# Attention outputs scaled before the transposes, summed in one PSUM group and left transposed

## The chip, the cores and the metric

The kernel runs on one core of a Trainium2 chip. The metric is the device time of one execution in microseconds; lower is better. The engines are TensorE (PE; its weight loads are PEld), VectorE (DVE), ScalarE (ACT), GpSimd (POOL) and SyncE (SP), which issues transfers.

## What is computed

One layer of a decoder on 1024 tokens of width 1024, in float32: a feed-forward, token mixing by attention, a feed-forward, each followed by a normalisation. Of the mixing, what matters here (cut to its core):

```python
# group A, sparse: 8 heads in 2 groups, 64 wide, query tiles of 128; three branches
p_cmp = masked_softmax(qb @ k_cmp * scale)          # 63 compressed keys
p_sel = masked_softmax(qb @ k_sel * scale)          # all blocks up to the tile
p_win = masked_softmax(qb @ kwb * scale)            # the last 512 keys and the tile's own
gates = sigmoid(gate_logits)
o = gates[..., 0:1] * (p_cmp @ v_cmp) + gates[..., 1:2] * (p_sel @ v_sel) + gates[..., 2:3] * (p_win @ vwb)
# group B, latent: 8 heads, queries and keys 96 wide, values 64, causal
p = masked_softmax((qn @ k_nope + qr @ k_rope) * scale)
o = p @ v
# both: the heads' outputs side by side (1024 columns) @ w_out, gated, added to alpha * x
# masked_softmax(s): e = exp(s - max), 0 where masked; e / max(sum(e), 1e-30)
```

## The kernel before

`sparse_attention` and `latent_attention` build lists of units and give them to `attend`. A unit is 512 query rows as four rows of 128 (in the sparse part four heads of one tile, in the latent part four tiles of one head) against its blocks of keys: in the sparse part 48 units (2 groups x 8 tiles x 3 branches, in the order selection, window, compressed), with 1 to 8 blocks of 128 keys for the selection, 1 to 5 for the window and one of 64 for the compressed branch, 132 blocks of 128 in all; in the latent part 16 units (8 heads x 2 halves) with 4 and 8 blocks. For each unit:

- *score*: PE makes the scores in PSUM, DVE their negated maximum, ACT the exponentials into `exps`, with their sums.
- *turn*, once a block: PE transposes the block's exponentials into one of three ring banks (`BANKS`); ACT rounds them into `turned_hi`; DVE subtracts into `turned_lo` (L2805) and so frees the bank.
- *apply*, once a block: PE multiplies the value matrix with `turned_hi` and with `turned_lo` into `out_ps` (L2735). The value matrix holds 64 columns of high parts and 64 of low parts, so `out_ps` has two halves of 64 rows, each an output, transposed.
- *finish*, once a unit: ACT copies `out_ps` to `out_sb` (L2769), PE transposes it back by four transposes into a ring bank (L2741), DVE adds the two halves (L2816) and inverts the floored sums (L2809, L2813), POOL multiplies by the factor, and in the sparse part by the gate, and adds the branch to `h` (L2829 to L2842).

Three rooms hold exponentials in the sparse part, one for each branch, and four in the latent part. POOL also scales the latents' columns in the first 16 units (L2915).

`plan` writes each engine's order by a list schedule: it gives every step a price (`pe_price` and so on), and picks on each engine the head of a stream that can start first; between those that can start equally soon the tuple in the call decides (`"pe": (1, 2, 0, 0)` for scoring, turning, applying, finishing: applying and finishing come first). Each engine then runs its order and waits on semaphores that count steps.

After the latent attention, `modulated_transpose` (stage `turn3`) transposes all of `h`'s 8 output chunks on PE into `u_hi` and `u_lo` for the output projection. `project` then takes `w_out` in chunks of 128 rows: DVE multiplies a chunk by the gate row (L2003), ACT rounds it (L1983), DVE subtracts (L2006), and PE does 8 x 3 matmuls for it (L2044). The chunks and the gate row are requested at the start of `turn3`, the rows of x behind them.

## Time and profile before

| | us |
|---|---|
| median of 3 runs (2226.71 to 2231.69) | 2229.32 |
| the profiled execution, whole | 2232.52 |
| its span | 2230.7 |
| PE busy in the span | 2115.3 (95%) |
| DVE busy | 1508.7 (68%) |
| ACT busy | 1001.9 (45%) |
| POOL busy | 599.0 (27%) |

The sparse attention stands at 924 to 1218 us of the span, the latent inputs at 1218 to 1273, the latent attention at 1273 to 1449, `turn3` at 1449 to 1462, the output projection up to 1554, the second feed-forward behind it. Matmuls are pipelined: an instruction's duration overlaps the next one's, so what one costs PE is better read from start to start. The mean in a row of groups is one instruction's; the busy time beside it counts overlapping parts once.

### The profile page before, as it was taken

Reading aid. Unit: us, or ns where it says so; the run is one execution under the profiler, and the core shown is the slowest. Engines: PE = TensorE matmul, PEld = TensorE weight load, DVE = VectorE, ACT = ScalarE, POOL = GpSimd, SP = SyncE. Lnnn points to the kernel's source line nnn. Section 1 sums busy time; section 2 is a strip of 40 time slices with the busy share of each in tenths; the row PEclk is TensorE's granted clock in tenths of the full one; section 3 lists DMA queues with packets and bytes.
Section 4 is the critical chain, followed back from the end, with each engine's and each line's share of the span. In section 5 each row is a group of like instructions: output and inputs, shape, how many; then the busy total and the mean of one; then the engine's idle time right before and its main releaser. Section 6 shows DMA issues by size and latency. Waiting matters only on the chain. (4 is left out here: it accounts for less than half of the span.)

```text
span 2230.7 us, 29121 instructions
## 1 busy us (share of the span) xinstructions
PE 2115.3 (95%) x10361; PEld 1771.7 (79%) x10361; DVE 1508.7 (68%) x2361; ACT 1001.9 (45%) x1925; POOL 599.0 (27%) x597
## 2 busy tenths in 40 slices
PE   5999999999999999799998899998999999999997
PEld 4888888878887887688886789877788888887885
DVE  6877777766886414687887577744765555558689
ACT  3433333334554112887886467621733323324443
POOL 0366656611100000132312000000245555540301
PEclk9999999999998999799999899989999999999998
DMA  7255544468831310300000000041333333347975
GB/s 268 88 168 170 166 165 162 168 206 267 249 109 56 126 46 18 117 1 1 1 1 1 1 1 1 1 151 36 112 118 113 104 118 109 105 127 259 293 258 100
DMA packets 193638, 254.46 MB, mean 114 GB/s; under 512 B 18192, under 2 KB 116560, under 8 KB 193495
## 3 DMA queue, kind: packets, MB, share of 16 engines
q1 hardware_dynamic: 178088, 208.04, 28.1%
q0 software_dynamic: 15408, 44.57, 7.7%
q8 instruction: 83, 1.36, 0.2%
q14 instruction: 59, 0.48, 0.1%
HBM read 212.72 MB, written 43.52 MB: 115 GB/s over the span
## 5 line engine op out<-in xcount | busy, mean ns | idle before, releaser
L781 DVE TENSOR_TENSOR ffn2A_u<-ffn2A_u,ffn_banks 128x512 f32<-128x512 f32 x60 | 41.2, 687 | 118.5 <-PE ffn_banks L725 112.4
L2757 ACT ACTIVATE nsaa_exps<-nsaa_scores,nsaa_neg_max 128x64 f32<-128x64 f32 (+8 forms) x192 | 108.3, 578 | 23.5 <-DVE nsaa_neg_max L2790 15.1
L2805 DVE TENSOR_TENSOR nsaa_turned_lo<-nsaa_ring,nsaa_turned_hi 128x512 fp32r<-128x512 f32 (+1 forms) x148 | 96.7, 683 | 23.4 <-ACT nsaa_turned_hi L2766 22.2
L1315 DVE SCALAR_TENSOR_TENSOR late_part_late<-ada_rows,far_silu_c,late_part_late 128x1024 f32<-128x1024 f32 x56 | 107.2, 1914 | 3.3 <-DMA ada_rows<-in_w_ada 3.2
L602 ACT ACTIVATE ffn1A_t_hi<-ffn1A_t 128x512 fp32r<-128x512 f32 x80 | 48.5, 628 | 132.2 <-POOL ffn1A_t L595 100.3
L602 ACT ACTIVATE ffn2A_t_hi<-ffn2A_t 128x512 fp32r<-128x512 f32 x80 | 48.4, 628 | 122.1 <-POOL ffn2A_t L595 93.8
L2044 PE MATMUL in_acc<-mix_in_w_hi,mix_in_u_hi 128*128 128x494 f32 x256 | 99.4, 388 | 0.7 <-PEq L85 0.7
L2044 PE MATMUL in_acc<-mix_in_w_lo,mix_in_u_hi 128*128 128x494 f32 x256 | 99.1, 387 | 0.0
L2044 PE MATMUL in_acc<-mix_in_w_hi,mix_in_u_lo 128*128 128x494 f32 x256 | 99.0, 387 | 0.0
L725 PE MATMUL ffn_banks<-ffn1S_s_hi,ffn1A_t_hi 128*128 128x512 f32 x240 | 93.8, 391 | 0.0
L725 PE MATMUL ffn_banks<-ffn1S_s_hi,ffn1A_t_lo 128*128 128x512 f32 x240 | 93.4, 389 | 0.0
L725 PE MATMUL ffn_banks<-ffn2S_s_hi,ffn2A_t_hi 128*128 128x512 f32 x240 | 93.4, 389 | 0.0
L725 PE MATMUL ffn_banks<-ffn1S_s_lo,ffn1A_t_hi 128*128 128x512 f32 x240 | 93.4, 389 | 0.0
L725 PE MATMUL ffn_banks<-ffn2S_s_lo,ffn2A_t_hi 128*128 128x512 f32 x240 | 93.4, 389 | 0.0
L725 PE MATMUL ffn_banks<-ffn2S_s_hi,ffn2A_t_lo 128*128 128x512 f32 x240 | 93.4, 389 | 0.0
L2766 ACT ACTIVATE nsaa_turned_hi<-nsaa_ring 128x512 fp32r<-128x512 f32 (+1 forms) x148 | 83.3, 599 | 20.1 <-PE nsaa_ring L2725 19.3
L2725 PE MATMUL nsaa_ring<-all_ident,nsaa_exps 128*128 128x128 f32 (+1 forms) x592 | 82.9, 275 | 2.7 <-DVE nsaa_turned_lo L2805 2.5
L2006 DVE TENSOR_TENSOR mix_in_w_lo<-mix_in_w_raw,mix_in_w_hi 128x494 fp32r<-128x494 f32 x28 | 18.8, 672 | 97.4 <-ACT mix_in_w_hi L1983 97.4
L619 DVE TENSOR_TENSOR ffn2A_t_lo<-ffn2A_t,ffn2A_t_hi 128x512 fp32r<-128x512 f32 x80 | 73.8, 945 | 13.9 <-ACT ffn2A_t_hi L602 12.9
L781 DVE TENSOR_TENSOR ffn1A_u<-ffn1A_u,ffn_banks 128x512 f32<-128x512 f32 x60 | 41.0, 684 | 58.5 <-PE ffn_banks L725 58.5
L2725 PEld LDWEIGHTS nsaa_ring<-all_ident,nsaa_exps 128*128 128x128 f32 (+1 forms) x592 | 68.1, 138 | 11.0 <-DVE nsaa_turned_lo L2805 4.2
L997 PE MATMUL ffn_banks<-ffn2B_d_hi 128*128 128x512 f32 x188 | 73.6, 392 | 2.5 <-ACT ffn2R_p L1040 1.7
(643 smaller groups left out, 6921.2 us busy)
## 6 DMA issues: line engine op xcount, KB each, us to landing
ada_rows<-in_w_ada POOLq DMA_DIRECT2D x56, 512.0 KB, 4.7
ffn_raw_g<-in_ffn_wg SPq DMA_DIRECT2D x44, 512.0 KB, 3.7
ffn_raw_u<-in_ffn_wu SPq DMA_DIRECT2D x44, 512.0 KB, 4.9
early_w<-in_w_ada SPq DMA_DIRECT2D x16, 512.0 KB, 7.0
mix_in_w_raw<-in_w_in SPq DMA_DIRECT2D x32, 247.0 KB, 2.6
ffn_rest<-in_ffn_wd SPq DMA_DIRECT2D x29, 256.0 KB, 5.0
hidden<-ffn1A_c SPq DMA_DIRECT2D x22, 256.0 KB, 4.5
hidden<-ffn1A_u SPq DMA_DIRECT2D x22, 256.0 KB, 5.0
```

Of the source, the lines that this page charges most:

```text
L602: act.activation(self.b_hi[w][:, :], self.block_of(w), ACT.Copy).then_inc(self.rounded, 1)
L619: dve.tensor_tensor(self.b_lo[w][:, :], self.block_of(w), self.b_hi[w][:, :].bitcast(F32), ALU.subtract).then_inc(self.split, 1)
L725: last = pe.matmul(out, b[w][:, cols], u[a][:, c, :], start=(not joins and c == 0 and m == 0), stop=(c == KC - 1 and m == 2), skip_group_c ...
L781: dve.tensor_tensor(out, base, bank, ALU.add).then_inc(self.mixed, 1)
L997: last = pe.matmul(self.banks[:, 4 * QUAD[p] + i, :], h[:, rows], w[:, HALF:D], start=(j == 0 and at == 0 and not JOINS[p]), stop=(j == PA ...
L1315: dve.scalar_tensor_tensor(out=part_late[:, v, :], in0=ada[:, n % 2, :], scalar=silu_c[:, k:k + 1], in1=part_late[:, v, :], op0=ALU.mult, ...
L2006: dve.tensor_tensor(lo[:, k, :], raw[:, k, :], hi[:, k, :].bitcast(F32), ALU.subtract).then_inc(split, 1)
L2044: last = pe.matmul(acc[:, i, 0:width], u[:, c, i * P:(i + 1) * P], w[:, c % slots, :], start=(c == 0 and m == 0), stop=(c == DC - 1 and m ...
L2725: last = pe.transpose(bank[0:u.keys, r * P:(r + 1) * P], exps[n % slots][:, r, k * u.keys:(k + 1) * u.keys], ident[:, :])
L2757: made = act.activation(u.kept(r, exps[n % slots]), u.seen(r, scores[:, m % 2, :]), ACT.Exp, bias=neg_max[:, n % SUMS, r:r + 1], accum_out ...
L2766: act.activation(turned_hi[0:u.keys, j % copies, cols], bank[0:u.keys, cols], ACT.Copy).then_inc(hi_done, 1)
L2805: dve.tensor_tensor(turned_lo[0:u.keys, j % copies, cols], bank[0:u.keys, cols], turned_hi[0:u.keys, j % copies, cols].bitcast(F32), ALU.s ...
```

## The change

The exponentials of a block are multiplied by their row's factor (1 / sum, in the sparse part gate / sum) in place, before the turn. In the sparse part POOL does every block; in the latent part's long units DVE does the first three blocks (`by_vector`) and POOL the others. The gate goes into the floored sum as 1 + exp(-x), which `sparse_inputs` now makes instead of the sigmoid. So the three branches of a tile add up in one PSUM group. *Finish* is gone; *fold* takes its place, once a tile and group (16 times) or once a latent unit (16 times): ACT copies one half of `out_ps`'s rows across to `other`, and DVE adds the other half and writes the sum, still transposed, into `h`. The compressed branch's values stand twice, on 128 partitions, and the low part of its turned block goes to the lower 64 rows of `turned_hi`, so that one matmul applies both. Each branch has two rooms, some of them unused columns of `h`. `turn3` is gone: `project` makes `u_hi` and `u_lo` from `h` chunk by chunk, and requests the chunks, the gate row and then x itself. The scaling of the latents moves from POOL to DVE. The streams' order on PE becomes scoring, turning, applying.

```diff
-def modulated_transpose(nc, stage, x_sb, shift, scale, ident, u_hi, u_lo, ahead, reload=None, arrives=None):
...
 def project(...):
+            if reload is not None:
+                chunks.ahead(sp)
             load(0, slots)
+            if reload is not None:
+                for i in range(TT):
+                    sp.dma_start(out[:, i, :], reload[i * P:(i + 1) * P, :]).then_inc(out_in[0], 16)
...
+                if u_raw is not None and n == 0:
+                    act.activation(u_hi[:, c, :].rearrange("p (i q) -> p i q", q=P), u_raw[c], ACT.Copy).then_inc(u_hi_done, 1)
...
+                if u_raw is not None and n == 0:
+                    dve.wait_ge(u_hi_done, c + 1)
+                    dve.tensor_tensor(u_lo[:, c, :].rearrange("p (i q) -> p i q", q=P), u_raw[c],
+                                      u_hi[:, c, :].bitcast(F32).rearrange("p (i q) -> p i q", q=P), ALU.subtract).then_inc(u_split, 1)
...
 def plan(...):
         elif kind == "turn":
-            found.append(("act", last_score[n]))
+            found.append(("dve" if k < u.by_vector else "pool", ("weigh", n, u.weighed_with(k))))
         elif kind == "apply":
             found.append(("dve", ("turn", n, k)))
-            if k == 0 and n:
-                found.append(("act", ("apply", n - 1, len(units[n - 1].blocks) - 1)))
-            if is_last(x) and n:
-                found.append(("pe", ("finish", n - 1, 0)))
+            if k == 0 and u.opens and u.group:
+                found.append(("dve", fold_of[u.group - 1]))
...
 def attend(...):
-                    if k == 0 and n:
-                        pe.wait_ge(out_moved, n)
-                    for m, part in enumerate((turned_hi, turned_lo)):
-                        last = pe.matmul(out_ps[:, cols], u.value_of(u.blocks[k]), part[0:u.keys, j % copies, cols],
-                                         start=(k == 0 and m == 0), stop=(k == len(u.blocks) - 1 and m == 1))
+                    if k == 0 and u.opens and u.group:
+                        pe.wait_ge(folded, u.group)
+                    start, stop = u.opens and k == 0, u.closes and k == len(u.blocks) - 1
+                    if u.one_block:
+                        last = pe.matmul(out_ps[:, :], u.value_of(0), turned_hi[:, j % copies, :], start=start, stop=stop)
+                    else:
+                        pe.matmul(out_ps[:, cols], u.value_of(u.blocks[k]), turned_hi[:, j % copies, cols], start=start, stop=False)
+                        last = pe.matmul(out_ps[:, cols], u.value_of(u.blocks[k]), turned_lo[:, j % copies, cols], start=False, stop=stop)
...
-                    for r in range(4):
-                        last = pe.transpose(bank[:, r * P:(r + 1) * P], out_sb[:, r, :], ident[:, :])
...
+                elif kind == "factor":
+                    b = n % SUMS
+                    dve.wait_ge(exped, last_score[n] + 1)
...
+                        dve.scalar_tensor_tensor(out=floor[:, b, :], in0=sums[:, b, :], scalar=1e-30, in1=u.gate,
+                                                 op0=ALU.max, op1=ALU.mult).then_inc(floored, 1)
...
+                elif kind == "weigh":
+                    dve.wait_ge(factored, n + 1)
+                    for r in range(4):
+                        at = u.room[:, r, 0:min(u.widths[r], u.by_vector * u.keys)]
+                        last = dve.tensor_scalar(at, at, factor[:, n % SUMS, r:r + 1], None, ALU.mult)
+                    last.then_inc(weighed_dve, 1)
+                elif kind == "fold":
+                    dve.wait_ge(moved, u.group + 1)
+                    folding.dve(dve, u.group, out_ps, other).then_inc(folded, 1)
...
+                top = u.weighed_rows(k)
+                at = u.room[:, top:4, k * u.keys:(k + 1) * u.keys]
+                by = factor[:, n % SUMS, top:4].unsqueeze(2).to_broadcast([P, 4 - top, u.keys])
+                pool.tensor_tensor(at, at, by, ALU.mult).then_inc(weighed_pool, 1)
...
-        attend(nc, stage + "a", units, Staging(), ident, ident_r, 3, 6, {"pe": (1, 2, 0, 0), "act": (2, 0, 1), "dve": (1, 0, 2)}, 0,
-               ahead=ahead, beside=scale_latents)
+        attend(nc, stage + "a", units, Staging(), Folding(), ident, ident_r, 6,
+               {"pe": (0, 1, 2), "act": (2, 0, 1), "dve": (2, 1, 0, 0, 3), "pool": (0,)}, 0, ahead=ahead, beside=scale_latents)
```

PE's order in the sparse attention, around the application of a compressed unit, before (`nsaa_ring<-all_ident,nsaa_exps` is a turn, `nsaa_out_sb` a finish, `sparse_vc` the compressed values):

```order
L2725 MATMUL nsaa_ring<-all_ident,nsaa_exps 128x128 x4
L2741 MATMUL nsaa_ring<-all_ident,nsaa_out_sb 128x128 x4
L2725 MATMUL nsaa_ring<-all_ident,nsaa_exps 128x128 x4
L2735 MATMUL nsaa_out_ps<-nsaa_turned_hi,sparse_vc 128x512
L2735 MATMUL nsaa_out_ps<-nsaa_turned_lo,sparse_vc 128x512
```

and now, at such a place (the rooms are named `nsa_exps` or lie in `h_h`):

```order
L2757 MATMUL nsaa_out_ps<-nsaa_turned_hi,sparse_v 128x512
L2758 MATMUL nsaa_out_ps<-nsaa_turned_lo,sparse_v 128x512
L2744 MATMUL nsaa_ring<-all_ident,nsa_exps 128x128 x4
L2744 MATMUL nsaa_ring<-all_ident,nsa_exps 64x128 x4
L2755 MATMUL nsaa_out_ps<-nsaa_turned_hi,sparse_vc 128x512
L2744 MATMUL nsaa_ring<-all_ident,nsa_exps 128x128 x4
```

The finish is gone from between the turns, and one matmul applies the compressed block.

DVE's order at the end of the latent attention and the start of the projection, before:

```order
L2809 TENSOR_SCALAR mlaa_floor<-mlaa_sums 128x4
L2813 RECIPROCAL mlaa_factor<-mlaa_floor 128x4
L2816 TENSOR_REDUCE h_h<-mlaa_ring 128x4x64
L85 UNCONDITIONAL_BRANCH
L215 UNCONDITIONAL_BRANCH
L174 TENSOR_TENSOR mix_out_u_lo<-turn_tp,mix_out_u_hi 128x512 x16
L85 UNCONDITIONAL_BRANCH
L1997 UNCONDITIONAL_BRANCH
L2003 TENSOR_TENSOR w_out_w_raw<-w_out_w_raw,w_out_gate 128x512
L2006 TENSOR_TENSOR out_w_lo<-w_out_w_raw,out_w_hi 128x512
```

and now, from the last long unit's factor on:

```order
L2829 TENSOR_SCALAR mlaa_floor<-mlaa_sums 128x4
L2836 RECIPROCAL mlaa_factor<-mlaa_floor 128x4
L2841 TENSOR_SCALAR mla_exps<-mla_exps,mlaa_factor 128x384 x4
L3045 TENSOR_TENSOR h_h<-mlaa_out_ps,mlaa_other 64x4x128
L2823 TENSOR_TENSOR mlaa_turned_lo<-mlaa_ring,mlaa_turned_hi 128x512 x5
L2823 TENSOR_TENSOR mlaa_turned_lo<-mlaa_ring,mlaa_turned_hi 128x384
L2823 TENSOR_TENSOR mlaa_turned_lo<-mlaa_ring,mlaa_turned_hi 128x256
L2823 TENSOR_TENSOR mlaa_turned_lo<-mlaa_ring,mlaa_turned_hi 128x128
L3045 TENSOR_TENSOR h_h<-mlaa_out_ps,mlaa_other 64x4x128
L86 UNCONDITIONAL_BRANCH
L1973 UNCONDITIONAL_BRANCH
L1979 TENSOR_TENSOR w_out_w_raw<-w_out_w_raw,w_out_gate 128x512
```

Factor and four scalings now stand ahead of the unit's turned blocks, the fold stands last, and the 16 subtractions of the turning stage are gone. Behind the last row DVE does a chunk of 128x1024 (`mix_out_u_lo<-h_h,mix_out_u_hi`) and then the weights' low half, for each chunk.

## Rows read from the trace of the kernel before

**Rows 1.** Busy time by stretch: us, then each engine's busy (count), PE clock, DMA share, GB/s
```profile
940.00:1205.00 265.00, 254.00 (x1684) 218.02 (x1682) 221.77 (x412) 209.80 (x565) 72.48 (x130) 1.00 0.00 1
...
924.00:1217.00 293.00, 275.23 (x1784) 234.91 (x1784) 237.96 (x444) 226.59 (x614) 78.36 (x143) 0.98 0.03 9
...
1273.00:1300.00 27.00, 23.85 (x122) 20.20 (x121) 15.47 (x27) 14.50 (x34) 0.61 (x1) 0.81 0.00 1
1300.00:1449.00 149.00, 144.63 (x943) 129.58 (x941) 113.63 (x217) 102.85 (x243) 9.20 (x15) 1.00 0.00 1
1449.00:1464.00 15.00, 9.82 (x64) 9.60 (x64) 10.82 (x17) 9.15 (x17) 0.00 (x0) 0.73 0.86 327
1464.00:1555.00 91.00, 89.11 (x384) 73.37 (x384) 30.35 (x49) 9.48 (x16) 0.00 (x0) 0.97 0.14 45
```

**Rows 2.** Waits, 924 to 1217: who for whom, us in total, times, longest
```profile
PEld nsaa_out_ps L2735 <- DVE nsaa_turned_lo L2805: 12.7, 26, 1.5
```

**Rows 3.** Timeline of PE, 1100 to 1112: start, duration, what
```profile
1106.35 0.63 PE L2741 MATMUL nsaa_ring<-all_ident,nsaa_out_sb 128*128 128x128 f32 x4
1106.91 0.50 PE L2735 MATMUL nsaa_out_ps<-nsaa_turned_hi,sparse_vc 64*128 64x512 f32 x1
1107.24 0.39 PE L2735 MATMUL nsaa_out_ps<-nsaa_turned_lo,sparse_vc 64*128 64x512 f32 x1
1107.57 0.42 PE L2712 MATMUL nsaa_scores<-sparse_k_hi,nsa_q 128*128 128x320 f32 x1
```

**Rows 4.** PE's groups of finish: count, then busy us, mean ns, idle before
```profile
L2741 PE MATMUL nsaa_ring<-all_ident,nsaa_out_sb 128*128 128x128 f32 x192 | 29.3, 275 | 2.6 <-ACT nsaa_out_sb L2769 1.6 <-DVE nsaa_joined L2816 0.5 <-DVE nsa_q L2879 0.4
...
L2741 PE MATMUL mlaa_ring<-all_ident,mlaa_out_sb 128*128 128x128 f32 x64 | 9.6, 273 | 0.8 <-ACT mlaa_out_sb L2769 0.8
```

**Rows 5.** DVE's and ACT's groups, shapes apart, same columns
```profile
L2816 DVE TENSOR_REDUCE nsaa_joined<-nsaa_ring 128x256 f32<-128x512 f32 x48 | 32.0, 666 | 5.0 <-PE nsaa_ring L2741 5.0
...
L2879 DVE SCALAR_TENSOR_TENSOR nsa_q<-nsaa_ring,nsa_q 64x256 fp32r<-64x256 f32 x32 | 13.5, 422 | 6.3 <-ACT nsa_q L2874 5.8
...
L2971 DVE TENSOR_TENSOR mla_k_lo<-mlaa_ring,mla_k_hi 64x512 fp32r<-64x512 f32 x16 | 10.9, 682 | 15.8 <-ACT mla_k_hi L2966 15.8
...
L2379 DVE TENSOR_TENSOR latent_ukv_lo<-latent_w_ukv,latent_ukv_hi 128x1024 fp32r<-128x1024 f32 x2 | 2.4, 1220 | 2.9 <-ACT latent_ukv_hi L2359 2.9
...
L172 DVE CAST queries_q_hi<-latent_in_u 128x512 fp32r<-128x512 f32 x4 | 1.7, 420 | 0.3 <-ACT latent_in_u L158 0.3
...
L619 DVE TENSOR_TENSOR ffn2A_t_lo<-ffn2A_t,ffn2A_t_hi 128x512 fp32r<-128x512 f32 x80 | 73.8, 945 | 13.9 <-ACT ffn2A_t_hi L602 12.9
...
L2769 ACT ACTIVATE nsaa_out_sb<-nsaa_out_ps 128x512 f32<-128x512 f32 x48 | 28.8, 599 | 17.8 <-PE nsaa_out_ps L2735 17.3
```

**Rows 6.** POOL's groups over the whole span, shapes apart, same columns
```profile
L595 POOL TENSOR_TENSOR ffn1A_t<-ffn_raw_g,ffn1A_t 128x512 f32<-128x512 f32 x20 | 40.4, 2020 | 1.6
...
L828 POOL TENSOR_TENSOR ffn2A_c<-ffn2A_c,ffn2A_silu 128x512 f32<-128x512 f32 x20 | 31.7, 1584 | 6.8 <-DVE ffn2A_c L779 6.8
...
L824 POOL TENSOR_TENSOR ffn1A_u<-ffn1A_u,ffn1A_c 128x512 f32<-128x512 f32 x20 | 25.8, 1288 | 64.7 <-ACT ffn1A_c L791 64.7
L2840 POOL TENSOR_TENSOR h_h<-h_h,nsaa_joined 128x256 f32<-128x256 f32 x32 | 23.4, 731 | 2.5
...
L2837 POOL TENSOR_TENSOR nsaa_joined<-nsaa_joined,nsaa_factor_g 128x256 f32<-128x256 f32 x32 | 19.6, 613 | 14.2 <-DVE nsaa_joined L2816 14.2
```

**Rows 7.** Timeline from the last latent work to the projection, PE, then DVE
```profile
1446.32 0.63 PE L2741 MATMUL mlaa_ring<-all_ident,mlaa_out_sb 128*128 128x128 f32 x4 [0.78 <-ACT mlaa_out_sb L2769]
1449.57 9.82 PE L145 MATMUL turn_tp<-all_ident,h_h 128*128 128x128 f32 x64 [2.62 <-PEq L3002]
1464.78 0.80 PE L2044 MATMUL out_acc<-out_w_hi,mix_out_u_hi 128*128 128x512 f32 x1 [5.40 <-DVE out_w_lo L2006]
...
1462.65 0.69 DVE L2003 TENSOR_TENSOR w_out_w_raw<-w_out_w_raw,w_out_gate 128x512 f32<-128x512 f32 x1 [0.40 <-PEq L85]
```

**Rows 8.** DMA issues, 1449 to 1475: count, KB each, median us to landing
```profile
w_out_gate<-gate_rows SPq DMA_DIRECT2D x1, 512.0 KB, 4.6
```

295 lines of the change are left out of this document (156 added, 139 removed).

## The prediction

> **What bounds the kernel now.** I read the busy time of each engine in stretches first [rows 1]. The change touches three stretches: the sparse attention (924 to 1217 us of the span), the latent attention (about 1273 to 1449) and what lies between it and the output projection (1449 to 1464, then the projection). The reader is to see that TensorE (PE) is busy 254.0 of 265 us in the middle of the sparse attention and 144.6 of 149 us in the latent one, while VectorE (DVE) has 221.8 and 113.6, ScalarE (ACT) 209.8 and 102.9, and GpSimd (POOL) only 72.5 and 9.2. So PE sets the pace of both, DVE is next, at 84% and 76%, and POOL is nearly free. The waits say the same [rows 2]: PE's longest is 12.7 us in 26 times, its weight loads for DVE's low halves. In 1449 to 1464 PE works 9.8 of 15 us and its clock is granted at 0.73: a stage of its own that turns the heads' outputs, with nothing beside it.
>
> **The sparse attention, PE.** Each of the 48 units (8 tiles x 2 groups x 3 branches) has a "finish" of four transposes; all go. In the stretch shown, the finish that starts at 1106.35 holds PE until 1106.91, 0.56 us [rows 3]. The whole group is 29.3 us busy, 0.61 each, with ends that overlap what follows [rows 4]. Where a finish stands next to other transposes the handover is shared, so I take 0.5: 48 x 0.5 = 24 us (17 to 29). The compressed branch's two applications with 64 rows become one with 128: from 1106.91 to 1107.57 the pair takes 0.66 [rows 3], half of it goes, 16 x 0.33 = 5 us. PE loses 29 us of work and gains none.
>
> **The sparse attention, DVE and ACT.** DVE loses 48 reductions, 32.0 us [rows 5]. It keeps the floor (now with the gate in it) and the reciprocal. It gains 32 fold additions of 64 x 256 from PSUM; the nearest row, L2879, has the same shape, 422 ns: 13.5 us. It takes over from POOL the 16 scalings of the latents, 128 x 384 and 128 x 256 in SBUF; the nearest is the cast of 128 x 512 at 420 ns, so about 0.35 each, 5 us. Net 32.0 - 18.5 = 13.5 less: 238.0 becomes 224.5. ACT loses 48 copies of 599 ns, 28.8 us, and gains 32 of half the columns, at most 19 us [rows 5]. Neither comes near PE in work. But with PE 29 us shorter, DVE's share of the stage rises from 81% (238.0 of 293) to 85% (224.5 of 264), and the places where PE waits for DVE get more frequent. I give back 4 us for this (0 to 13, the upper end below).
>
> **The sparse attention, POOL.** This is the unknown. POOL now multiplies every block of exponentials by its row's factor, and a turn waits for that. There are 132 blocks of 128 x 512 and 16 of 128 x 256; before, no such row with 512 columns exists. The same form at 256 columns takes 613 ns and, with a strided second operand, 731 [rows 6]: doubled, 1.23 and 1.46. A sum of two 512-column tiles in the feed-forward takes 1288, others 1584 and 2020 [rows 6]. The last two stand beside DVE instructions with two inputs in SBUF (L619, 945 ns for 512 columns that L2971 does in 682 [rows 5]); in the attention DVE reads one operand from PSUM, and there POOL's 613 is steady. I take 1.25: 132 x 1.25 + 16 x 0.61 = 175 us in a stage of 268. It is hidden under PE as long as it runs ahead, and two things let it: each branch has two rooms for its exponentials where it had one, and scoring has the first right on PE. What shows is one fill at the start (floor, reciprocal and one block, 1.6 us before the first turn) and less at the end: the old tail behind the last application (copy 0.60, four transposes, reduction 0.67, two POOL steps 0.61 and 0.73) is 3.1 us, the new one two copies and two additions of 0.42, about 1.8. The two cancel. So the sparse attention gives 29 - 4 = 25 us, plus about 1 for the copies that held the one output bank (three serial rounds at its end); 26 in all.
>
> The Trainium skill, in "GPSIMD Engine Reference", section 4.1 (Engine selection), speaks against this part: it puts elementwise work on VectorE and calls GPSIMD about half as fast for two inputs. The row agrees on the rate, since 613 ns for 256 columns is 2.4 ns a column where DVE's subtraction of 512 columns takes 0.68 (L2971 [rows 5]). By the rule the blocks would go to DVE, whose 224.5 us would then pass PE's work; here the engine with 72.5 us in 265 is the one to take them.
>
> **One group a tile.** The three branches now add up in one PSUM group, and the bank is closed 16 times instead of 48. A closing costs more: ACT's copy and DVE's additions must both be over before the next tile's first application, 1.8 us instead of 0.6. PE fills that with scores and turns (6 copies in the sparse attention, 4 in the latent one), so I price it inside the 4 us.
>
> **The latent attention.** PE loses 16 finishes, 9.6 us busy [rows 4]; at 0.5 each, 8 us. DVE loses 16 reductions of 0.67, 10.7 us, and gains 16 folds of 64 x 512 (682 ns in the nearest row [rows 5], 10.9 us) and 32 scalings of 128 x 384 (0.35, 11 us): 11 us more. Its share rises from 76% to 88% (124.8 of 141). This is the same share that DVE has beside a full PE in no row, so I give back 3: 5 us gained (-7 to 8). POOL has 8 heads x 3072 columns, at 2.4 ns 59 us of 170, hidden. The first blocks of a long unit go to DVE (four scalings, 1.4 us) while POOL does the later ones.
>
> **Between latent attention and output projection.** The last transposes of the old tail start at 1446.32, the turning stage at 1449.57, the projection at 1464.78 [rows 7]. The turning stage goes. The old tail behind the last application becomes a copy and an addition, about 1.4 us shorter, so the projection's stage starts near 1448.1. There its gate row and weights must land, which the turning stage hid: 4.6 us from issue [rows 8]. Then DVE does the gate product 0.69 (the row at 1462.65), the low half of the activations, 128 x 1024 from SBUF, 1.22 as in L2379 [rows 5], and the low half of the weights 0.69; with 0.3 for handovers the first matmul stands at 1455.6, 9 us earlier. Later chunks need 2.6 us of DVE each against 5.5 of PE (24 matmuls, 0.23 each) and hide. PE starts after some 9 idle us, so its first matmuls run at the lower clock level, as now; I take 1 us off: 8 gained (5 to 10).
>
> **Before the sparse attention** the values of the compressed branch are copied twice and the gates take an exponential, with an addition behind it on DVE: about 1 us lost at a stage boundary.
>
> **The sum.** 26 + 5 + 8 - 1 = 38 us. The profiled execution took 2232.5 us (span 2230.7), so 2194.5 for it; the median of the three runs, 2229.3, lies 3.2 lower, and the prediction is 2191. With all terms at their good ends (29 + 5, 8, 10, -1) it is 2178; with the give-backs at their bad ends but POOL hidden about 2205.
>
> **Rivals.**
> - *DVE becomes the bound.* For it: DVE feeds back every PSUM bank and PE's own waits are for it. If its share could not rise at all, the sparse stage would be 224.5 / 0.81 = 277 (16 gained) and the latent one, where DVE now works 15.5 + 113.6 = 129.1 of 176 us, 140 / 0.73 = 191 (15 lost): 16 - 15 + 7 = 8, 2221. Against: 84% stands in the middle of the sparse stage with PE at 96%. Half-way gives 2207.
> - *POOL becomes the bound.* A stage of 267 us with some 16 for fill and tail leaves 251, so from (251 - 10) / 132 = 1.83 us a block the stage follows POOL. At 2.02, the slowest row, it is 132 x 2.02 + 12 + 16 = 295, nothing gained, and the whole is about 2217. The Trainium skill's "GPSIMD Engine Reference", section 8 (Key points), says that GPSIMD shares its SBUF interfaces with VectorE and suffers beside DVE instructions in a two-port mode or with two SBUF inputs. By that rule the scalings of the latents, and in the latent attention those of the blocks, would hold POOL up; they are 5 and 11 us, so only a little.
> - *Slower than before.* The same mechanism further: the feed-forward's 2.02 us, times 731 / 613 for operands that lie strided in h, is 2.41 us; the sparse stage is then 132 x 2.41 + 14 + 16 = 348, 55 lost, 2229 + 55 - 12 = 2272. It decides from 2.1 us a block, where the sparse stage loses the 12 gained elsewhere. Against: 613 ns holds in the very stage.
> - *Better.* If twice the rooms remove PE's present waits too (12.7 us [rows 2]), the result is 2177 to 2180.
>
> **Chances.** Forecast as it stands (2180 to 2201) 0.58; better 0.08; DVE the bound (2201 to 2221) 0.17; POOL the bound but not slower 0.08 (0.03 of it within 0.2%), slower by it 0.08; 0.01 for the new starts and tails eating all. The range 2176 to 2214 leaves out about 2 in 10. A measurement of this kernel can tell about 0.2%, 4.5 us, from no change; within that lie 0.04, faster 0.88, slower 0.08.
>
> **What will show it.** Sparse stage from 293 to about 267 with PE still above 93% busy; POOL's 128 x 512 rows at 1.2 to 1.3 us; PE waits for POOL under 5 us in total; DVE at 85%. Latent stage near 170. First projection matmul about 7 us after the last latent work instead of 18. Wrong if POOL's rows stand above 1.8, if PE's waits for DVE double, or if PE waits for the fold at the start of a tile.

## The result and the profile after

The changed kernel takes 2246.4 us (median of 6 runs, 2239.8 to 2253.2) against 2230.2 for the one before (6 runs, 2226.7 to 2232.0): ratio 1.0072, 95% interval 1.005 to 1.0093. It is slower by 0.7%, where 2191 was forecast, in a range of 2176 to 2214. The profiled execution took 2248.2 us, with a span of 2246.2.

First the busy time by stretch, the columns as in [rows 1]: the sparse attention from its first scores to the last write of its output, then the latent attention, from its first matmul to the same end; below them the same two stretches of the kernel before, cut at the same events.

```profile
929.40:1207.90 278.50, 250.91 (x1574) 216.67 (x1574) 237.79 (x442) 214.03 (x594) 142.66 (x148) 0.96 0.02 8
...
1263.60:1470.10 206.50, 178.95 (x1000) 153.80 (x1000) 161.67 (x276) 120.40 (x276) 55.74 (x72) 0.90 0.00 1
```
```profile
926.90:1218.10 291.20, 274.56 (x1782) 234.60 (x1782) 237.12 (x442) 224.71 (x611) 79.38 (x144) 0.98 0.02 8
1272.70:1448.40 175.70, 168.78 (x1064) 150.08 (x1064) 129.10 (x244) 117.35 (x276) 9.78 (x16) 0.97 0.00 1
```

The sparse attention is 13 us shorter, not 26. The latent attention is 31 us longer, where 5 were to be gained. In both, read the length less PE's busy time, PE's idle time: it goes from 16.6 to 27.6 us in the sparse attention and from 6.9 to 27.5 in the latent one. PE's clock is granted at 0.90 of full speed in the latent stage, 0.97 before.

What PE waits for in the latent attention of the kernel after (who for whom, us in total, times, longest):

```profile
PE mlaa_ring L2744 <- DVE mla_exps L2841: 21.6, 8, 5.3
```

That is one wait in each of the eight long units, for VectorE's scalings of the exponentials. The groups of the kernel after that answer to [rows 5] and [rows 6]: count, then busy us, mean ns of one, idle before.

```profile
L2841 DVE TENSOR_SCALAR mla_exps<-mla_exps,mlaa_factor 128x384 f32<-128x384 f32 x32 | 32.0, 1058 | 0.3
...
L2816 DVE TENSOR_SCALAR nsaa_neg_max<-nsaa_neg_max 128x4 f32<-128x4 f32 x16 | 7.6, 474 | 0.5
...
L2925 DVE TENSOR_SCALAR h_h<-h_h,sparse_rstd 128x384 f32<-128x384 f32 x8 | 4.2, 519 | 0.0
...
L2945 DVE TENSOR_TENSOR h_h<-nsaa_out_ps,nsaa_other 64x256 f32<-64x256 f32 x32 | 13.4, 418 | 3.0 <-ACT nsaa_other L2938 2.7
```
```profile
L2856 POOL TENSOR_TENSOR nsa_exps<-nsa_exps,nsaa_factor 128x512 f32<-128x512 f32 x80 | 80.7, 1043 | 113.1 <-DVE nsaa_factor L2836 113.1
...
L2856 POOL TENSOR_TENSOR mla_exps<-mla_exps,mlaa_factor 128x512 f32<-128x512 f32 x16 | 17.2, 1097 | 96.5 <-DVE mlaa_factor L2836 96.5
```

GpSimd is faster than feared: 1043 ns for a block of 128x512. The folds take 418 ns, as priced. But VectorE's scaling of 128x384 takes 1058 ns, priced at 350, and the timeline of one long unit shows beside what (start, us, engine, what):

```profile
1339.29 0.18 DVE L2836 RECIPROCAL mlaa_factor<-mlaa_floor 128x4 f32<-128x4 f32 x1
1339.50 4.00 DVE L2841 TENSOR_SCALAR mla_exps<-mla_exps,mlaa_factor 128x384 f32<-128x384 f32 x4
1339.54 4.21 POOL L2856 TENSOR_TENSOR mla_exps<-mla_exps,mlaa_factor 128x512 f32<-128x512 f32 x5 [12.70 <-DVE mlaa_factor L2836]
1343.41 0.67 DVE L3013 TENSOR_TENSOR mla_k_lo<-mlaa_ring,mla_k_hi 64x512 fp32r<-64x512 f32 x1
```
```profile
1343.64 0.63 PE L2744 MATMUL mlaa_ring<-all_ident,mla_exps 128*128 128x128 f32 x4 [2.22 <-DVE mla_exps L2841]
```

VectorE's four scalings and GpSimd's five products begin together and end together, 4.0 and 4.2 us long. Behind the wait PE's clock falls: 1.00 from 1325 to 1339.5, 0.79 from 1343.7 to 1352, in parts of it the lower of the two levels.

```profile
1325.00:1339.50 14.50, 14.50 (x90) 12.56 (x89) 11.41 (x22) 9.72 (x24) 1.85 (x4) 1.00 0.00 0
1343.70:1352.00 8.30, 8.30 (x46) 7.33 (x47) 6.81 (x14) 5.71 (x13) 2.81 (x5) 0.79 0.01 3
```

The boundary that answers to [rows 7] is as forecast. The last fold starts at 1469.38, the projection at 1479.08: 9.0 us after the last latent work, where it was some 16.

```profile
1469.38 0.69 DVE L3045 TENSOR_TENSOR h_h<-mlaa_out_ps,mlaa_other 64x512 f32<-64x512 f32 x1 [1.25 <-ACT mlaa_other L3039]
...
1476.60 0.69 DVE L1979 TENSOR_TENSOR w_out_w_raw<-w_out_w_raw,w_out_gate 128x512 f32<-128x512 f32 x1 [6.52 <-DMA w_out_w_raw<-in_w_out]
...
1479.08 0.80 PE L2026 MATMUL out_acc<-out_w_hi,mix_out_u_hi 128*128 128x512 f32 x1 [10.35 <-DVE out_w_lo L1986]
```

### The profile page after: what moved, and what is told of

Same layout as the page of the kernel before. It is cut to its first block and busy times, and to the rows that moved or that the text cites. A ratio compares the mean times of both kernels' runs of the same rounds, so it can differ in the third digit from the quotient of the medians.

```text
span 2246.2 us, 28288 instructions
## 1 busy us (share of the span) xinstructions
PE 2093.4 (93%) x10025; PEld 1749.0 (78%) x10025; DVE 1543.6 (69%) x2387; ACT 992.7 (44%) x1901; POOL 707.0 (31%) x657
## 5 line engine op out<-in xcount | busy, mean ns | idle before, releaser
L2856 POOL TENSOR_TENSOR nsa_exps<-nsa_exps,nsaa_factor 128x512 f32<-128x512 f32 (+1 forms) x96 | 90.4, 972 | 120.5 <-DVE nsaa_factor L2836 120.5
L2783 ACT ACTIVATE nsaa_turned_hi<-nsaa_ring 128x512 fp32r<-128x512 f32 (+1 forms) x148 | 85.3, 599 | 35.0 <-PE nsaa_ring L2744 24.8
L2823 DVE TENSOR_TENSOR nsaa_turned_lo<-nsaa_ring,nsaa_turned_hi 128x512 fp32r<-128x512 f32 x132 | 87.9, 683 | 14.3 <-ACT nsaa_turned_hi L2783 12.3
L2774 ACT ACTIVATE nsa_exps<-nsaa_scores,nsaa_neg_max 128x64 f32<-128x64 f32 (+8 forms) x136 | 71.8, 542 | 21.2 <-DVE nsaa_neg_max L2807 16.2
L965 PE MATMUL ffn_banks<-ffn1B_d_hi 128*128 128x512 f32 x188 | 73.3, 390 | 1.2 <-ACT ffn1R_p L1008 1.1
```

The lines of the kernel that those rows point to most:

```text
L965: last = pe.matmul(self.banks[:, 4 * QUAD[p] + i, :], h[:, rows], w[:, HALF:D], start=(j == 0 and at == 0 and not JOINS[p]), stop=(j == PA ...
L2774: made = act.activation(u.kept(r, u.room), u.seen(r, scores[:, m % 2, :]), ACT.Exp, bias=neg_max[:, n % SUMS, r:r + 1], accum_out=sums[:, ...
L2783: act.activation(turned_hi[0:u.keys, j % copies, cols], bank[0:u.keys, cols], ACT.Copy).then_inc(hi_done, 1)
L2823: dve.tensor_tensor(low, bank[0:u.keys, cols], turned_hi[0:u.keys, j % copies, cols].bitcast(F32), ALU.subtract).then_inc(ring_free, 1)
L2856: pool.tensor_tensor(at, at, by, ALU.mult).then_inc(weighed_pool, 1)
```

## The experiments

Line numbers in diffs are left out; all edits are in the functions shown above. A stretch of a stage is cut at the same events as above.

### The latent attention: who weighs, and when

**One: GpSimd weighs all blocks.**
```
-                        None, before, 3, 1360, 3 * half, rooms[2 * b + half])
+                        None, before, 3, 1360, 0, rooms[2 * b + half])
```


> One number is changed: in the latent attention GpSimd weighs every block of the exponentials, and VectorE none; all else is as in the changed kernel. Theory A (VectorE's four 128x384 scalings, 1.0 us each beside GpSimd's multiplications instead of the 0.35 us of the prediction, hold back the first turn of a unit and everything behind it): the first turn then waits for one multiplication of GpSimd, about 1.1 us, instead of 4.0 us; PE's waits at the first line of the turn, 35 us of the stage, fall under 15; the latent attention goes from 207 us to 175 to 185 and the kernel from 2246 to 2218 to 2228 us. Theory B (it is the order of the steps: every turn now stands behind a factor, whatever engine weighs): the waits stay, because GpSimd must weigh eight blocks in a row, 6.5 us against 4.0, and the stage stays at 203 us or more, the kernel at 2243 or more.


Measured: 2222.0 us, ratio 0.9973 (0.9958 to 0.9989); the latent attention takes 184.2 us. Both are as theory A had them.

**Two: GpSimd starts when VectorE is through.** Only a wait is added.
```
             pool.wait_ge(factored, n + 1)
+            if u.by_vector:
+                pool.wait_ge(weighed_dve, weigh_no["weigh", n, 0] + 1)
```


> One wait is added: in the long units of the latent attention GpSimd begins with its blocks only when VectorE is through with its four scalings of 128x384. So the two never weigh at the same time. Theory A (the two exclude each other): the mean of the scalings falls from 1058 ns to 0.3 to 0.45 us, the four from 4.0 to under 1.8 us, PE's first turn comes 2.2 us or more earlier in eight units, GpSimd ends no later than now by more than 1.5 us a unit, and the stage gets shorter by 8 to 18 us: the kernel at 2228 to 2238 us. Theory B (VectorE's scaling of 128x384 is as slow as this by itself): the scalings stay at 1.0 us, and GpSimd's blocks come 4 us later, so the stage gets longer by 5 us or more.


Measured: 2210.5 us, ratio 0.9927 (0.9902 to 0.9952), lower than both theories had it. The stretch of the latent attention, then VectorE's scalings and the same place in a timeline:

```profile
1260.10:1434.60 174.50, 165.09 (x1000) 140.34 (x1000) 140.36 (x276) 118.95 (x276) 52.05 (x72) 0.98 0.00 1
```
```profile
L2841 DVE TENSOR_SCALAR mla_exps<-mla_exps,mlaa_factor 128x384 f32<-128x384 f32 x32 | 11.3, 416 | 0.3
```
```profile
1306.37 1.41 DVE L2841 TENSOR_SCALAR mla_exps<-mla_exps,mlaa_factor 128x384 f32<-128x384 f32 x4
1307.92 3.75 POOL L2858 TENSOR_TENSOR mla_exps<-mla_exps,mlaa_factor 128x512 f32<-128x512 f32 x5 [12.95 <-DVE mla_exps L2841]
```

One after the other they need 1.41 and 3.75 us, 5.3 with the handover; at once, 4.2. So sending GpSimd off later costs it 1.1 us and brings VectorE's blocks, which PE turns first, 2.6 us earlier. Adding a wait takes 32 us from the stage. PE's idle time falls by 18.1 of them (27.5 to 9.4 us); the other 13.9 are PE's busy time, for the same 1000 matmuls at a granted clock of 0.98 instead of 0.90. So the gain is larger than the eight waits alone.

**Three: no weighing at all.** The steps of GpSimd and VectorE are left out and a turn waits for the factor.
```
-                    if k < u.by_vector:
-                        pe.wait_ge(weighed_dve, weigh_no["weigh", n, 0] + 1)
-                    else:
-                        pe.wait_ge(weighed_pool, weigh_no["weigh", n, k] + 1)
+                    pe.wait_ge(factored, n + 1)
```


> Nothing is weighed, in either attention: the multiplications of GpSimd and of VectorE are left out (the outputs lack the factors), the factors are still computed, and a turn waits for the factor alone. This is the price of all weighing. Theory A: the latent attention at 165 to 172 us (the 176 of the kernel before less its finishes, 5 to 8), VectorE's small instructions in the sparse attention back at their 170 ns beside the kernel before (floor 187 instead of 259 ns, the mask's minimum 192 instead of 474), the sparse attention at 268 to 275 us instead of 282, the kernel at 2190 to 2205 us. Theory B (the order with its waits costs, not the weighing): latent attention still 195 us or more, sparse attention still 280, the kernel at 2232 or more.


Measured: 2202.3 us, ratio 0.9889 (0.9866 to 0.9912). The latent attention takes 172.5 us, 2 less than with the added wait, so all of the 31 us were the collision. The sparse attention takes 266.0, less than expected, to which the third part returns.

**Four: VectorE weighs all of a long unit** (`8 * half` in the line of the first).


> One number is changed: in the latent attention VectorE weighs all eight blocks of a long unit (four scalings of up to 128x1024) and GpSimd only the four of the short ones. GpSimd is idle beside most of VectorE's scalings. Theory A: without GpSimd beside it VectorE scales 128x1024 in 0.6 to 0.8 us, four rows of 640 to 1024 columns in under 2.8 us, where now four of 384 take 4.0; the stage gets shorter by 5 to 20 us, the kernel at 2226 to 2241 us. Theory B (VectorE is slow at this by itself, 1.0 us for 384 columns): 2.2 us or more for each scaling, 9 us a unit, PE waits 5 us longer in each of the eight long units, the stage 230 us or more, the kernel at 2270 or more.


Measured: 2221.4 us, ratio 0.9967 (0.9951 to 0.9982), latent attention 181.6 us. The scalings, 832 columns on the mean, take 650 ns (18.7 us for 32): VectorE isn't slow at this. The kernel is faster than theory A had it (2226 to 2241), as in the second.

All four fit the exclusion in kind, two with a gain above its range. The second theories, order or a slow VectorE, fall: the order was the same in the second experiment.

### What is shut out

**Five and six: operands that don't lie side by side.** In the fifth, on top of the second, the small tiles are interleaved; in the sixth, without the added wait, the wide scalings go over even and odd columns.
```
-        sums = s.sb("sums", [P, SUMS, 4])
-        neg_max = s.sb("neg_max", [P, SUMS, 4])
-        floor = s.sb("floor", [P, SUMS, 4])
-        factor = s.sb("factor", [P, SUMS, 4])
+        both = s.sb("sums", [P, SUMS, 8])
+        sums, floor = both[:, :, 0:8:2], both[:, :, 1:8:2]
+        pair = s.sb("neg_max", [P, SUMS, 8])
+        neg_max, factor = pair[:, :, 0:8:2], pair[:, :, 1:8:2]
```


> On top of the added wait of the run before (VectorE's scalings first, then GpSimd: 2210 us), only the layout of the small tiles is changed: the four sums, floors, maxima and factors of a unit stand two elements apart instead of side by side. Theory A2 (VectorE's instructions that read and write side-by-side SBUF in its fast form are the ones that GpSimd's multiplications shut out): with a stride the minimum of the mask goes from 490 to about 170 to 200 ns and the floor from 273 to 160 to 200 ns; at most 8 us less of VectorE in the sparse attention, of which the path shows 2 to 6: kernel 2203 to 2209 us. Theory B2 (any two SBUF operands are shut out, whatever their layout): both stay at 450 and 260 ns or more, kernel within 3 us of 2210.


Measured: 2216.5 us, ratio 0.9933 (0.9916 to 0.9949); floor 280 ns, the mask's minimum 495 (273 and 490 in the second experiment): no change in the instructions. The kernel is 6 us above the second experiment's 2210.5, outside what either theory said; the two intervals overlap, and the cause of these 6 us stays open.
```
-                        at = u.room[:, r, 0:min(u.widths[r], u.by_vector * u.keys)]
+                        at = u.room[:, r, 0:min(u.widths[r], u.by_vector * u.keys)].rearrange("p (c two) -> p two c", two=2)
```


> No added wait: against the changed kernel only the access pattern of VectorE's four scalings in the latent attention is changed, first the even columns of the 384, then the odd ones, in the same instruction. Theory A2 (the fast form is what is shut out): each takes 0.42 to 0.55 us though GpSimd multiplies beside it, the four 2.0 us instead of 4.0, the latent attention is at 180 to 190 us instead of 207 and the kernel at 2220 to 2230 us. Theory B2 (any SBUF-to-SBUF instruction of VectorE waits for GpSimd): 1.0 us each as before, and the kernel at 2243 or more.


Measured: 2241.4 us, ratio 1.0064 (1.0042 to 1.0086); the scalings take 1060 ns, as in the changed kernel. A stride of two doesn't free an instruction. It doesn't show either which property of it is what counts.

**Seven and eight: four forms side by side.** VectorE's four wide instructions get four forms, beside GpSimd (the changed kernel) and alone (with the added wait).
```
+                        by = factor[:, n % SUMS, r:r + 1]
+                        if r == 0:
+                            last = dve.tensor_copy(at, at)
+                        elif r == 1:
+                            last = dve.tensor_tensor(at, at, by.to_broadcast([P, at.shape[1]]), ALU.mult)
+                        elif r == 2:
+                            last = dve.reciprocal(at, floor[:, n % SUMS, r:r + 1].to_broadcast([P, at.shape[1]]))
+                        else:
+                            last = dve.tensor_scalar(at, at, by, None, ALU.mult)
```


> The changed kernel, but VectorE's four scalings of 128x384 in the latent attention have four forms: row 0 a copy onto itself, row 1 a product with the factor as a second tensor, row 2 a reciprocal of a small operand, row 3 the scaling as it was. It leaves rows 0 and 2 unweighed, so the output is wrong. All stand beside GpSimd's multiplications. Theory B2 (any instruction of VectorE on SBUF alone is shut out): all four at 0.8 us or more. Theory C (it depends on the form): the reciprocal runs at its own pace, about 0.4 us, as the one of 128x4 does (178 ns in every kernel), and the copy, the product and the scaling at 0.8 us or more.

> The same four forms with the added wait, so that GpSimd is idle beside them: the pace of each form alone, against which the run before is read. Two rows are again left unweighed. The scaling at 0.35 to 0.45 us (416 ns before), the copy the same or less, the product and the reciprocal 0.4 to 0.5 us. If a form is as slow here as beside GpSimd, it isn't shut out but slow.


Measured, the forms' groups beside GpSimd, then alone:
```profile
L2847 DVE RECIPROCAL mla_exps<-mlaa_floor 128x384 f32<-128x384 f32 x8 | 20.3, 2540 | 0.0
L2845 DVE TENSOR_TENSOR mla_exps<-mla_exps,mlaa_factor 128x384 f32<-128x384 f32 x8 | 11.2, 1395 | 0.0
L2849 DVE TENSOR_SCALAR mla_exps<-mla_exps,mlaa_factor 128x384 f32<-128x384 f32 x8 | 3.5, 439 | 0.0
L2843 DVE COPY mla_exps<-mla_exps 128x384 f32<-128x384 f32 x8 | 2.9, 360 | 0.3
```
```profile
L2847 DVE RECIPROCAL mla_exps<-mlaa_floor 128x384 f32<-128x384 f32 x8 | 20.4, 2546 | 0.0
L2845 DVE TENSOR_TENSOR mla_exps<-mla_exps,mlaa_factor 128x384 f32<-128x384 f32 x8 | 4.4, 551 | 0.0
L2843 DVE COPY mla_exps<-mla_exps 128x384 f32<-128x384 f32 x8 | 2.9, 360 | 0.3
...
L2849 DVE TENSOR_SCALAR mla_exps<-mla_exps,mlaa_factor 128x384 f32<-128x384 f32 x8 | 2.6, 321 | 0.0
```
The product of two tensors goes from 551 to 1395 ns and the scaling from 321 to 439, though it meets only GpSimd's last, narrow product. The reciprocal takes 2.54 us either way, and GpSimd's products run on beside it: the one of 128x384 takes 820 ns there and 826 with VectorE idle. The copy isn't slowed; here it is GpSimd that is held up, and its products of 128x512, of which the first meets the copy and the second the product of two tensors, take 1280 ns on the mean instead of 1039:
```profile
1336.30 0.36 DVE L2843 COPY mla_exps<-mla_exps 128x384 f32<-128x384 f32 x1
1336.35 4.23 POOL L2864 TENSOR_TENSOR mla_exps<-mla_exps,mlaa_factor 128x512 f32<-128x512 f32 x5 [12.18 <-DVE mlaa_factor L2836]
```
```profile
L2864 POOL TENSOR_TENSOR mla_exps<-mla_exps,mlaa_factor 128x512 f32<-128x512 f32 x16 | 20.2, 1280 | 90.7 <-DVE mlaa_factor L2836 90.7
```
Who starts first doesn't decide it: the copy starts 0.05 us ahead of GpSimd's product and keeps its 360 ns, and the scaling of the changed kernel starts 0.04 us ahead of it (1339.50 and 1339.54 above) and takes 1.30 us. No run shows why. Neither theory had it whole: it depends on the form, and the reciprocal is slow by itself, 2.5 us where I expected some 0.4. These two runs measured the forms, not the kernel's time (2247.0 and 2235.0 us, one execution each).

The Trainium skill has the rule, in "SBUF — State Buffer", section "Who interferes with whom": VectorE and GpSimd share one pair of SBUF ports as an exclusive lock, held for a whole instruction; VectorE asks for it with copies and scalings in a two-port mode and with two inputs in SBUF. The trace agrees in this: a copy, scalings and products hold GpSimd up or are held up by it, by the numbers above; reciprocals aren't (2540 and 2546 ns), and neither are the two forms seen here that read PSUM (the fold, 418 ns beside GpSimd's work and 419 without any, and the low half of a turned block, 683 and 686). The prediction used a shorter form of this rule, which doesn't have the word "exclusive".

### The sparse attention

Here VectorE has the same trouble in small. One of 17 cases over 450 ns, in the kernel after (of 64 floors and minima): a minimum over four numbers, 170 ns by itself, starts 0.06 us behind a product of GpSimd and ends 0.02 us after it. So it is in all 17: the end comes 0.02 to 0.03 us after that of the product that GpSimd had in hand.

```profile
1014.78 1.05 POOL L2856 TENSOR_TENSOR nsa_exps<-nsa_exps,nsaa_factor 128x512 f32<-128x512 f32 x1
1014.84 1.01 DVE L2816 TENSOR_SCALAR nsaa_neg_max<-nsaa_neg_max 128x4 f32<-128x4 f32 x1
```

**Nine: the latents' scalings back on GpSimd**, on top of the second experiment.
```
-                    if beside is not None:
-                        beside(dve, n)
...
             pool.wait_ge(factored, n + 1)
+                if beside is not None and k == 0:
+                    beside(pool, n)
```


> On top of the added wait (2210 us), the sixteen scalings of the latents in the sparse attention go from VectorE back to GpSimd, where the kernel before had them, each ahead of the first weighing of its unit. Theory A: VectorE is rid of 9.5 us that stood partly behind GpSimd, and GpSimd gets 16 instructions of 1.2 to 1.6 us more, of which the path sees those ahead of a first turn: sparse attention 275 to 281 us (now 278), kernel 2206 to 2213 us. If VectorE's busy time sets the sparse attention (227 of 260 us in its middle), it gains 5 us or more: 2205 or less. If GpSimd's latency sets it, it loses 5 or more: 2215 or more.


Measured: 2205.3 us, ratio 0.9901 (0.9875 to 0.9927), sparse attention 271.3 us. The expectation that comes nearest is the one in which VectorE's busy time sets the stage. It is the fastest version that leaves nothing out, 24 us ahead of the kernel before in the same series (2229.7) and 41 ahead of the changed kernel's 2246.4. The interval overlaps that of the second experiment (0.9902 to 0.9952), so the 5 us between those two are not settled. Of the 6.8 us by which the stage is shorter than there (278.1), PE's idle time gives only 2.3 (28.4 to 26.1); the rest is PE's busy time, at a granted clock of 0.98 instead of 0.97 (more on this under the thirteenth).

**Ten and eleven: the planner's price.** `u.keys * 2.9` becomes `u.keys * 1.85`, first on top of the second experiment, then on top of the ninth.


> On top of the added wait (2210 us), the planner's price of a weighing by GpSimd falls from 2.9 to 1.85 ns a column (1585 to 1047 ns for 128x512, which is what the trace shows), so the turns are put earlier on PE. If the rest of the lost time in the sparse attention (278 us, 266 without weighing) is order, it gains 3 to 8 us there: kernel 2202 to 2207 us. If it is VectorE's stretched instructions, it changes nothing: 2208 to 2213 us.

> The added wait, the latents' scalings back on GpSimd (together 2205 us), and the planner's price of GpSimd at 1.85 ns a column. Alone the two took 7 and 5 us from the sparse attention of 278 us. If they shorten the same wait, together they give no more than 7: 271 us, the kernel at 2203 to 2207. If they are separate, the sparse attention comes to 266 to 268 us, as without any weighing, and the kernel to 2198 to 2202 us.


Measured: 2210.5 us, ratio 0.9908 (0.9891 to 0.9925), and 2213.4, ratio 0.9935 (0.9922 to 0.9949). The tenth shortens the sparse attention from 278.1 to 273.4 us, PE's idle time in it from 28.4 to 24.8. Yet the kernel shows nothing: in the profiled execution the stage starts 2.0 us later, and the latent attention is 2.3 longer, at a granted clock of 0.96. Together the two aren't better: the eleventh lies above both of its expectations (at most 2207), with 274.1 us for the stage. With turns put earlier PE waits for GpSimd itself there:
```profile
PE nsaa_ring L2744 <- POOL nsa_exps L2858: 5.4, 11, 1.5
```

**Twelve: GpSimd in halves**, on top of the eleventh.
```
-                pool.tensor_tensor(at, at, by, ALU.mult).then_inc(weighed_pool, 1)
+                for r0, r1 in [(0, 2), (2, 4)] if top == 0 else [(top, 4)]:
+                    at = u.room[:, r0:r1, k * u.keys:(k + 1) * u.keys]
+                    by = factor[:, n % SUMS, r0:r1].unsqueeze(2).to_broadcast([P, r1 - r0, u.keys])
+                    last = pool.tensor_tensor(at, at, by, ALU.mult)
+                last.then_inc(weighed_pool, 1)
```


> As the run with both edits, but GpSimd weighs each block of four rows in two instructions of two rows (about 0.61 us each, the price of 128x256, instead of one of 1.04). If VectorE's small instructions wait for the end of the instruction that GpSimd has in hand, the longest of them falls from 1.0 to 0.6 us and the mean of the floor from 320 to about 240 ns; against it GpSimd works 20 to 25 us longer in the sparse attention (160 to 183 us). I expect the gain of VectorE (6 us, half of it on the path) and the loss by later turns (2 to 6 us) about even: within 4 us of the run with both edits. If VectorE's small instructions are slowed by something else in GpSimd's work, their mean stays at 320.


Measured: 2216.6 us, ratio 0.9945 (0.993 to 0.996), sparse attention 281.4 us. The kernel lies within the 4 us that were said, but what was expected of the floor fails: its mean rises from 345 to 408 ns and its longest from 1078 to 3511. The timeline of that one:
```profile
1151.68 4.62 POOL L2859 TENSOR_TENSOR nsa_exps<-nsa_exps,nsaa_factor 128x256 f32<-128x256 f32 x8
...
1152.80 3.51 DVE L2831 SCALAR_TENSOR_TENSOR nsaa_floor<-nsaa_sums,masks_gates 128x4 f32<-128x4 f32 x1
```
VectorE doesn't always get its turn between two products that follow each other at once. Of 15 floors and minima over 450 ns, 11 end with the product in hand or the next one, at 651 ns or less; four wait for several more and take 1785 to 3511. So shorter pieces shorten the usual wait and don't bound the longest. What decides between the two cases isn't shown.

**Thirteen: four blocks for VectorE** (`4 * half`, on top of the ninth).


> The best version so far, with four instead of three blocks of a long unit weighed by VectorE in the latent attention: four scalings of 128x512, about 0.39 us each against 0.32 to 0.36, and GpSimd four blocks instead of five. GpSimd starts 0.3 us later and ends 0.7 us earlier in each of eight units. The turns wait for neither now (2.8 us in the whole stage): no change, 2202 to 2208 us.


Measured: 2213.8 us, ratio 0.9925 (0.9908 to 0.9942), above the 2202 to 2208 expected; latent attention 178 us instead of 174, with the same idle time of PE (9.4 and 9.3 us) and a granted clock of 0.96 instead of 0.98. Not better; three blocks stay. But its sparse attention, the same code as in the ninth, serves as a control. The ninth and this one, busy time by stretch:

```profile
925.00:1196.30 271.30, 245.25 (x1574) 210.72 (x1574) 234.76 (x426) 213.13 (x594) 159.15 (x164) 0.98 0.02 8
```
```profile
927.70:1205.20 277.50, 251.31 (x1574) 215.77 (x1574) 235.05 (x426) 213.62 (x594) 159.38 (x164) 0.96 0.02 8
```

The same code takes 271.3 us at a granted clock of 0.98 and 277.5 at 0.96. PE's idle time is the same, 26.1 and 26.2; its busy time differs by 6.1 us. So the time at the lower level differs between executions of the same code, for a reason that no run shows, and a comparison of this stage needs the same clock, or goes by PE's idle time.

**Fourteen and fifteen: the small instructions left out**, with GpSimd at work (on top of the ninth) and without any weighing (on top of the third).
```
-                    if u.keys == CMP_PAD:
+                    if False:
...
-                        dve.scalar_tensor_tensor(out=floor[:, b, :], in0=sums[:, b, :], scalar=1e-30, in1=u.gate,
-                                                 op0=ALU.max, op1=ALU.mult).then_inc(floored, 1)
+                        dve.reciprocal(factor[:, b, :], sums[:, b, :]).then_inc(factored, 1)
```


> The best version so far (added wait, latents' scalings on GpSimd: 2205 us, sparse attention 271 us), but in the sparse attention VectorE's floor and the mask's minimum are left out, the two that wait for GpSimd (15.9 and 7.3 us there, 7.6 and 2.7 without GpSimd); the reciprocal, which does not wait, stays. It leaves out the gates, the floor and the guard of empty rows, so the output is wrong. If their waiting is on the path, the sparse attention comes to 263 to 266 us, and the kernel to 2196 to 2200. If the time goes by the wait for the weights, it stays at 269 us or more, the kernel at 2202 or more.

> The control of the run before: the same two instructions left out, and no weighing at all (as the run without weighing, sparse attention 266 us, 2202 us). Here they are short, 158 and 170 ns, 10 us together, beside 48 waits less. If their own work costs nothing, the stage stays at 264 to 267 us; if it is on the path, it is at 258 to 262 us. The difference of this step to the one with GpSimd at work is what the shutting out costs.


Measured: 2207.9 us, ratio 0.9902 (0.9881 to 0.9922), and 2201.0, ratio 0.9876 (0.9859 to 0.9892). The sparse attention of the fourteenth, the third and the fifteenth, in this order:

```profile
928.10:1198.80 270.70, 249.55 (x1574) 216.70 (x1574) 215.89 (x362) 212.66 (x594) 159.22 (x164) 0.96 0.02 8
```
```profile
925.60:1191.60 266.00, 244.67 (x1574) 212.27 (x1574) 226.62 (x442) 212.67 (x594) 0.00 (x0) 0.98 0.02 8
```
```profile
926.60:1194.20 267.60, 246.01 (x1574) 213.88 (x1574) 219.71 (x378) 212.29 (x594) 0.00 (x0) 0.97 0.02 8
```

By its own expectation the fourteenth speaks against a cost of the small instructions: 270.7 us is above 269, 2207.9 above 2202, and against the ninth (271.3) it looks like no gain. But it ran at 0.96, and the reading at one clock that follows was made after the result. Against the thirteenth, at the same 0.96, the stage is 6.8 us shorter (277.5 to 270.7) and PE's idle time falls from 26.2 to 21.2. Without weighing the same edit changes the idle time from 21.3 to 21.6, nothing. So with GpSimd at work the small instructions cost 5 to 7 us, and without it none; and with them gone, weighing costs PE no idle time (21.2 against 21.6). This rests on one profile of each kernel. The times of whole executions fit it where the clocks meet: at a mean granted clock of 0.970 the ninth took 2215.5 us and the fourteenth 2210.7.

## Why the prediction was wrong, point by point

**The latent attention** failed, at the step "32 scalings of 128 x 384 (0.35, 11 us)". By themselves they do take that: 1.41 us for four, 11.3 in all (416 ns each as the trace counts them, with ends that overlap). Beside GpSimd they take 32.0 us (1058 ns each). I had the work hidden beside "POOL does the later ones" and never asked whether the two can work at once. The step in the rivals failed with it: "they are 5 and 11 us, so only a little". That prices what VectorE does to GpSimd. The damage runs the other way: GpSimd's instructions are the long ones, and VectorE, which every turn waits for, stands behind them. Of the 31 us lost where 5 were to be gained, 20.6 are PE's idle time (6.9 to 27.5 us) and 10.2 its busy time (168.8 to 179.0), with 64 matmuls fewer, at a granted clock of 0.90 instead of 0.97. The second experiment gives back 32. VectorE's 11 us more of work were right where it is not shut out: 129.1 us before, 140.4 there. That is 80% of the stage; the 88% in the prediction set work of the whole stage against a part of it. The prediction's rows had a sign of the other direction too, 945 ns for VectorE's L619 beside GpSimd against 682 for L2971 [rows 5], and read it for GpSimd's sake alone; no run shows that it is the same lock.

**The latent finishes** were mis-sized as well. I took 8 us for 16 of them. In the third experiment PE's busy time falls from 168.8 to 164.3 us, 4.5 or 0.28 a finish, and the stage by 3.2 (175.7 to 172.5). With the added wait it is 174.5, so the change gains 1 here at best, not 5.

**The sparse attention** came out at 13 of 26 us. PE's work was right: 274.6 us busy before and 245.3 in the ninth experiment, both at a granted clock of 0.98, is 29.3 less, where 29 were forecast. In the kernel after it is 250.9, at 0.96: 5.7 us of the gain went to the lower clock level, as much as the same code shows between 0.98 and 0.96. The give-back of 4 us was too small: PE's idle time grew by 10.9, of which 4.7 stand without any weighing too (21.3 against 16.6), 4.9 are the small instructions shut out (26.1 against 21.2), and 1.3 are left. In sum 29.3 - 5.7 - 10.9 = 12.7.

**VectorE's load** was forecast to fall to 224.5 us in the sparse attention and stayed at 237.8. Part of it is the shutting out: 226.6 us without weighing.

**GpSimd** was right and better: 1043 ns for a block, forecast 1250; PE doesn't wait for it in the kernel after. The rival in which it becomes the bound, and the slower case built on it, are out. The kernel is slower by a mechanism that none of the rivals priced, though a sentence among them named it. "Slower" had 0.08, all of it for GpSimd as the bound; that the result falls there is luck and says nothing for that rival.

**The sum's bad end** was added up wrong. With the sparse attention at a give-back of 13 instead of 4 (17 us) and the latent one at -7, and the other terms as they were, the result is 17 - 7 + 8 - 1 = 17 us gained, 2212, not 2205. The measured 2246.4 lies outside either way.

**The boundary to the projection** was right: 9.0 us from the last latent work to the first matmul against 16.4, 7.4 us less where 8 stood (the sign to look for had been "about 7 us" instead of 18). **Before the sparse attention** the first scores come at 929.4 instead of 926.9; 1 was forecast, but that start lies between 925.0 and 931.3 us in the runs above, which are the same up to it.

**One group a tile** was right in kind: PE waits 7.3 us in 6 times for a fold, at the start of a tile. The prediction named this as a sign of error; it stands without weighing too (6.5 us), so it belongs to what the change costs without any collision, the 4.7 us above.

## What to carry to other kernels

When work goes to a second engine, price it beside what the first engine does at that moment, not by its duration alone, and price both directions: a short instruction of the critical engine behind a long one of the free engine. Where two engines can't work at once, put the one first whose result is awaited; an added wait made this kernel some 32 to 36 us faster (1.0072 to 0.9927 of the kernel before, 2246.4 to 2210.5 us in two series). And look in the profile for a duration that is far over the shortest of its own group: that can be a wait that no view of waits shows. Compare a stage at the same granted clock, or by PE's idle time.

## What the runs showed of the hardware

- VectorE and GpSimd hold each other up in SBUF, instruction by instruction: a VectorE minimum over 128x4, 170 ns alone, took up to 1014 ns behind one product of 128x512 (1043 ns on the mean).
- It depends on the form. Scaling (321 to 439 ns and, in the kernel after, 1058) and product (551 to 1395) are hit, a reciprocal isn't (2540 and 2546, and 172 to 179 for 128x4 everywhere), nor is the fold, which reads PSUM (418 and 419). A stride of two changes nothing (1058 and 1060). A copy kept its 360 ns, and GpSimd waited.
- VectorE may wait for several products in a row: 3511 ns behind instructions of 0.62 us each, where most waits ended with the product in hand.
- The same code of one stage took 271.3 us at a granted clock of 0.98 and 277.5 at 0.96, with the same idle time.
- A wide reciprocal is slow: 2.54 us for 128x384, 6.6 ns a column.
- A product of 128x512 on GpSimd takes 1040 ns with a broadcast factor, less than twice the 613 of 128x256 [rows 6].
